# The first attention of a two-layer trunk: biased logits written to SBUF, a longer pipeline, and query tiles taken in turn from both ends of a head

## The chip, the cores and the metric
One core of a Trainium2 chip runs the whole program in one launch. The time is the device time of that core in microseconds (us). Three runs of the kernel before gave 2849.36 to 2856.4 us, median 2853.4 us.

## The reference
The trunk has two layers over 2048 tokens of width 1024, in float32. Only the first attention of layer 0 (A) is touched, with the two stages behind it:

```python
s = einsum('bhmqd,bhmkd->bhmqk', q, k) * ATTN_SCALE + bias          # 4 heads, 2 maps m each, 64 deep
p = softmax(where(kpos // 64 <= qpos // 64, s, -inf), axis=-1)
attn = p[:, :, 0] - lam * p[:, :, 1]
o = einsum('bhqk,bhkd->bhqd', attn, v)                              # v is 128 wide
o = rms_norm(o, subln_g) * (1.0 - lam_init)
mixed = concatenate([a_out * silu(ag), b_out * silu(bg)])
y = mixed @ w_out_even
```

The bias depends on the distance alone. Beyond the last 256 keys in front of the diagonal it is constant over a row, and the kernel keeps only what differs from that.

## The kernel before, in words
The program is a chain of stages, each a block of its own with a barrier behind it: `project` (layer 0), `diff_attn` (attention A, tiles named a_), `band_attn` (B, b_), `output` (o_), and the same for layer 1 with attention C (c_). Every engine's order inside a stage is written by hand, and semaphores join the engines.

`diff_attn` (L534) goes through 64 steps `(h, i)`, 4 heads by 16 query tiles of 128 rows. The mask is causal, so step i has n = i + 1 key tiles of 128. In a head there are 136 key tiles. `steps` is in rising order of i. For each step g and each of the two maps m:

- TensorE (`qk`, L645) writes the negated logits into `logits`, 5 PSUM banks of 512 columns used in a ring, in ceil(n / 4) parts, two matmuls a part (high and low halves).
- VectorE (`maxima`) takes the minimum of each part but the last by a reduction (L709), joins them (L716), and adds the bias to the last part and folds its minimum in with one custom instruction (L720), which writes the part back to PSUM in place.
- ScalarE (`exponentials`, L770) takes one exponential a part out of PSUM into `prob` in SBUF, with a partial row sum each.

For the step as a whole VectorE (`difference`) sums the partial sums (L728), forms a ratio (L729, L730) and computes `prob0 + ratio * prob1`, 512 columns at a time (L734). TensorE transposes the result tile by tile (L658) into two `turned` banks, ScalarE copies those to `prob_t` (L778), TensorE multiplies by v (L671), VectorE scales the result into `out` (L739) and ScalarE takes its squares (L784). The loops are shifted against each other: in iteration g TensorE does `qk(g, 0)`, `pv(g - 2)`, `qk(g, 1)`, `transposes(g - 1)`, and VectorE does `maxima(g, 0)`, `difference(g - 1)`, `maxima(g, 1)`, `output(g - 2)`.

After the 64 steps comes a tail: the RMS factors of all 64 tiles (L752 to L754 and L80 to L83), 64 scalings by them (L757), 64 transposes (L689), 16 copies (L803) and 4 stores of 1 MB on SyncE's queue (L621).

The keys, queries and values of a head are loaded by SyncE's queue (L598 to L616), 13 DMAs for each block of 512 tokens, into two sets of buffers. Heads 0 and 1 are loaded at the start, head h + 2 when the products of head h are done. TensorE waits for block b of a head where it first needs it, at step i = 4b.

`output` (L1137) multiplies the concatenated heads by the gates and projects. For B the division by the row sums is made here: GpSimd widens the inverse sums to 512 columns (L1175), TensorE transposes them (`spreads`, L1290, 4 transposes a token tile; 8 in layer 1, where all 16 heads are such), and VectorE multiplies the gates by them (L1252).

## Time and profile before

| | us |
|---|---|
| median of three runs | 2853.4 |
| the profiled execution | 2854.47 |
| its span | 2852.8 |
| granted TensorE clock, mean of the span | 0.969 |
| first matmul of attention A to the first DMA of attention B | 650.26 to 1076.19 |

All sums below are made against the profiled execution, whose time is 1.7 us above its span. Busy time counts the instructions themselves; an engine that waits for another is idle. Matmul durations in a timeline overlap: the cost of one in a row of many is the distance between starts.

### The profile page before, as it was taken

The numbers are of one execution on the slowest core, as the hardware profiler recorded it, in microseconds if no ns is written. First come the engines' busy times: TensorE is split into PE (matmuls) and PEld (weight loads), VectorE is DVE, ScalarE is ACT, GpSimd is POOL, SyncE is SP. The second block draws the span as 40 slices with busy tenths as digits, with TensorE's granted clock in tenths as the row PEclk, the third lists the DMA queues.
The fourth block names the chain that finished last, engine by engine and source line by source line (L and its number), as shares of the span: only waits on it lengthen the run. The fifth ranks groups of instructions, "written<-read, shape, count | busy, mean of one in ns | idle before, by whom it ended". The sixth has DMA issues, their size and how long they took to land. (4 is left out here: it accounts for less than half of the span.)

```text
span 2852.8 us, 44070 instructions
## 1 busy us (share of the span) xinstructions
PE 2617.7 (92%) x16264; PEld 2231.2 (78%) x16264; DVE 1244.4 (44%) x2881; ACT 914.0 (32%) x2357; POOL 310.1 (11%) x199
## 2 busy tenths in 40 slices
PE   5999999987888885979969999999996999999898
PEld 4788888986676664768858888888996888888687
DVE  6411111107889873745531111111111777777465
ACT  4211111006777763622121111111001555555121
POOL 1121212100000003100012122121110000100100
PEclk9999999998999997989989999999998999999899
DMA  5344522129315009765463343321225676774652
GB/s 170 120 137 134 164 72 85 50 62 195 82 24 103 1 31 235 183 212 212 171 214 116 117 128 111 103 78 63 61 61 118 156 182 160 177 173 95 196 210 78
DMA packets 237932, 359.53 MB, mean 126 GB/s; under 512 B 59604, under 2 KB 136832, under 8 KB 237232
## 3 DMA queue, kind: packets, MB, share of 16 engines
q1 hardware_dynamic: 222800, 309.33, 39.2%
q0 software_dynamic: 11104, 41.95, 5.1%
q10 hardware_dynamic: 3840, 5.77, 0.9%
q8 instruction: 115, 1.88, 0.3%
q14 instruction: 73, 0.60, 0.1%
HBM read 223.75 MB, written 138.70 MB: 127 GB/s over the span
## 5 line engine op out<-in xcount | busy, mean ns | idle before, releaser
L520 PE MATMUL p_acc<-p_h_hi,p_w_hi 128*128 128x512 f32 x1440 | 565.1, 392 | 11.2 <-DVE p_h_lo L464 11.2
L520 PE MATMUL p_acc<-p_h_hi,p_w_lo 128*128 128x512 f32 x1440 | 562.0, 390 | 0.0
L520 PE MATMUL p_acc<-p_h_lo,p_w_hi 128*128 128x512 f32 x1440 | 561.9, 390 | 0.0
L520 PEld LDWEIGHTS p_acc<-p_h_hi,p_w_hi 128*128 128x128 f32 x1440 | 271.4, 188 | 69.9 <-DVE p_h_lo L464 14.5
L520 PEld LDWEIGHTS p_acc<-p_h_hi,p_w_lo 128*128 128x128 f32 x1440 | 271.1, 188 | 57.0
L520 PEld LDWEIGHTS p_acc<-p_h_lo,p_w_hi 128*128 128x128 f32 x1440 | 271.4, 188 | 55.3
L235 DVE SCALAR_TENSOR_TENSOR p_lo_out<-p_acc,p_hi_out 128x512 fp32r<-128x512 f32 x116 | 80.0, 691 | 486.7 <-ACT p_hi_out L219 486.6
L1108 ACT ACTIVATE c_prob<-c_logits,c_neg_max 128x640 f32<-128x640 f32 (+4 forms) x256 | 185.1, 727 | 206.2 <-DVE c_neg_max L1089 206.1
L1089 DVE CUSTOM_DVE_ANT_0 c_logits<-c_logits,c_bias 128x640 f32<-128x640 f32 (+4 forms) x256 | 185.8, 761 | 122.2 <-PE c_logits L1020 111.2
L219 ACT ACTIVATE p_hi_out<-p_acc 128x512 fp32r<-128x512 f32 x116 | 69.4, 598 | 511.0 <-PE p_acc L520 493.5
L517 PE MATMUL p_acc<-p_w_hi,p_h_lo 128*128 128x256 f32 (+1 forms) x768 | 224.0, 292 | 0.0
L517 PE MATMUL p_acc<-p_w_lo,p_h_hi 128*128 128x256 f32 (+1 forms) x768 | 224.0, 292 | 0.0
L517 PE MATMUL p_acc<-p_w_hi,p_h_hi 128*128 128x256 f32 (+1 forms) x768 | 224.0, 292 | 0.0
L1305 PE MATMUL o_acc<-w_out_hi,o_m_hi 128*128 128x512 f32 x512 | 204.4, 399 | 7.5 <-DVE o_m_lo L1256 7.5
L645 PE MATMUL a_logits<-a_k,a_q 128*128 128x512 f32 (+3 forms) x640 | 175.9, 395 | 37.1 <-DMA a_v<-scr_v_a 18.8
L770 ACT ACTIVATE a_prob<-a_logits,a_neg_max 128x512 f32<-128x512 f32 (+3 forms) x320 | 195.8, 624 | 34.8 <-DVE a_neg_max L720 33.7
L1305 PE MATMUL o_acc<-w_out_lo,o_m_hi 128*128 128x512 f32 x512 | 201.6, 394 | 0.0
L1305 PE MATMUL o_acc<-w_out_hi,o_m_lo 128*128 128x512 f32 x512 | 201.6, 394 | 0.0
L1020 PE MATMUL c_logits<-c_k,c_q 128*128 128x384 f32 (+2 forms) x960 | 176.3, 324 | 25.7 <-DMA c_v<-scr_v 24.6
L1020 PEld LDWEIGHTS c_logits<-c_k,c_q 128*128 128x128 f32 x960 | 147.0, 192 | 51.1 <-DMA c_v<-scr_v 25.4
L238 DVE TENSOR_TENSOR p_f_out<-p_acc,p_sig 128x512 f32<-128x512 f32 x64 | 44.2, 691 | 303.9 <-ACT p_sig L221 303.9
L1053 PE MATMUL c_o<-c_prob_t,c_v 128*64 128x128 f32 x2240 | 154.3, 279 | 0.1
(152 smaller groups left out, 4019.5 us busy)
## 6 DMA issues: line engine op xcount, KB each, us to landing
scr_qh<-p_hi_out SPq DMA_DIRECT2D x116, 256.0 KB, 2.5
scr_ql<-p_lo_out SPq DMA_DIRECT2D x116, 256.0 KB, 2.9
scr_gt<-p_f_out SPq DMA_DIRECT2D x128, 128.0 KB, 1.9
p_w_raw<-in_w_in_odd POOLq DMA_DIRECT2D x16, 1024.0 KB, 6.8
c_k<-scr_qh SPq DMA_DIRECT2D x60, 256.0 KB, 8.3
c_k<-scr_ql SPq DMA_DIRECT2D x60, 256.0 KB, 10.0
o_o<-scr_ot SPq DMA_DIRECT2D x6, 2048.0 KB, 8.7
o_g<-scr_gt SPq DMA_DIRECT2D x6, 2048.0 KB, 13.7
```

The source lines that it names most:

```text
L219: nc.scalar.activation(hi_out[:, buf, :], ps[:, :], ACT.Copy, scale=kind[1]).then_inc(act_done, 1)
L235: nc.vector.scalar_tensor_tensor(out=lo_out[:, buf, :], in0=ps[:, :], scalar=kind[1], in1=hi_out[:, buf, :].bitcast(F32), op0=ALU.mult, op ...
L238: nc.vector.tensor_tensor(f_out[:, buf, :], ps[:, :], sig[:, buf, :], ALU.mult).then_inc(dve_done, 1)
L517: last = nc.tensor.matmul(acc[v % 4][:, 0:n], ht[:, c, k * P:(k + 1) * P], wt[:, half, c * n:(c + 1) * n], **flags)
L520: last = nc.tensor.matmul(acc[v % 4][:, :], wt[:, half, c * n + cc * P:c * n + (cc + 1) * P], ht[:, c, b * BLK:(b + 1) * BLK], **flags)
L645: last = nc.tensor.matmul(logits[n % RING][:, 0:tiles * P], q, k_sb[h % 2][m][:, at * P:(at + tiles) * P], start=s == 0, stop=s == 1)
L770: nc.scalar.activation(prob[g % 2][m][:, at * P:(at + tiles) * P], logits[n % RING][:, 0:tiles * P], ACT.Exp, bias=neg_max[:, j:j + 1], sc ...
L1020: last = nc.tensor.matmul(s_ps[:, lo:hi], q_sb[b][:, i * P:(i + 1) * P], k_sb[b][s][:, tile * P:tile * P + hi - lo], start=s == 0, stop=s ...
L1053: last = nc.tensor.matmul(o_ps[half * HD:(half + 1) * HD, at:at + P], v_sb[:, j // TILES % 2, tile_of(j + half) - w + 1 + t, :], prob_t[:, ...
L1089: nc.vector.tensor_tensor_reduce(out=to, in0=s, in1=bias[:, b, WIDE - w * P:WIDE + SPARE], scale=1.0, scalar=HIGHEST, op0=ALU.add, op1=ALU ...
L1108: nc.scalar.activation(prob[:, j, 0:n], source, ACT.Exp, bias=neg_max[:, j:j + 1], scale=-1.0, accum_out=sums[:, h, tile_of(k):tile_of(k) ...
L1305: last = nc.tensor.matmul(acc[u % 4][:, :], mt[:, t % 2, c, :], wt[:, c, half * BLK:(half + 1) * BLK], start=step == 0, stop=step == 3 * K ...
```

## The change
In `diff_attn`:

- `logits` is now a ring of 3 parts of 1024 columns (6 banks), and `turned` is one bank in place of two.
- A map has one part for up to 8 key tiles and two above that. The last part has 8 tiles. Every part goes through the custom instruction, which now writes to `prob` in SBUF: the first part is added to `zeros`, the last to the bias, padded with zeros to 1024 columns. TensorE waits for `moved`, that is for VectorE, where it waited for the exponentials before.
- ScalarE makes one exponential for the whole row of a map, in place in SBUF, and its sum is the row sum.
- `difference` works on pieces of 1024 columns. `prob` of map 0 has three buffers.
- The loops are shifted further: `transposes(g - 2)` and `pv(g - 3)` alternate, four tiles at a time, with `qk(g, 1)` in the middle.
- The steps of a head are ordered 15, 0, 14, 1, ..., 8, 7; in head 0 they are 0, 1, 2, 3, then 15, 4, 14, 5, ..., 10, 9. TensorE waits for the blocks of a head where a step first needs them.
- `out` has 8 slots. Every 4 steps its tiles are transposed, copied with the gain and stored by four DMAs of 64 KB. Loads of head h + 2 stand behind the stores of head h on SyncE's queue.
- The tail is gone. The RMS factors are computed at the start of `band_attn` and applied in the first `output`, by widening them along with B's inverse sums: two GpSimd copies and 8 transposes a token tile instead of one and 4, and a gate product of 1024 columns instead of 512.

```diff
-        bias = st.sb("bias", [P, A_HEADS, BLK])
-        prob = [[st.sb(f"prob{b}{m}", [P, SEQ]) for m in range(2)] for b in range(2)]
+        PART = 2 * BLK
+        bias = st.sb("bias", [P, A_HEADS, PART])
+        zeros = st.sb("zeros", [P, PART])
+        prob = [[st.sb(f"prob{m}{b}", [P, SEQ]) for b in range(3 - m)] for m in range(2)]
         prob_t = st.sb("prob_t", [P, 2, SEQ])
-        out = st.sb("out", [P, A_HEADS * TILES, P])
+        SLOTS = 2 * TPB
+        out = st.sb("out", [P, SLOTS, P])
+        out_t = st.sb("out_t", [P, 2, BLK])
...
-        RING = 5
-        logits = [st.ps(f"logits{i}", [P, BLK]) for i in range(RING)]
-        turned = [st.ps(f"turned{i}", [P, BLK]) for i in range(2)]
+        RING = 3
+        logits = [st.ps(f"logits{i}", [P, PART]) for i in range(RING)]
+        turned = st.ps("turned", [P, BLK])
...
+        def mixed(first, last):
+            tiles = range(first, last)
+            return [i for pair in zip(reversed(tiles), tiles) for i in pair][:len(tiles)]
+
+        steps = [(h, i) for h in range(A_HEADS) for i in (list(range(TPB)) + mixed(TPB, TILES) if h == 0 else mixed(0, TILES))]
...
+                last = min(n, PART // P)
+                parts[g, m] = []
+                for at, tiles in [(0, n - last)] * (n > last) + [(n - last, last)]:
...
+            load(0)
+            load(1)
+            for n in range(G // TPB):
+                h, r = divmod(n, NBLK)
+                sp.wait_ge(out_left, n + 1)
+                for t in range(TPB):
+                    i = steps[n * TPB + t][1]
+                    sp.dma_start(scr["ot"][h * P:(h + 1) * P, i * P:(i + 1) * P], out_t[:, n % 2, t * P:(t + 1) * P]).then_inc(stored[n % 2], 16)
+                if r == NBLK - 1 and h + 2 < A_HEADS:
+                    sp.wait_ge(pv_done, TILES * (h + 1))
+                    load(h + 2)
...
+                if m == 0:
+                    for n in needs[g]:
+                        pe.wait_ge(head_loaded[h % 2][n], 16 * LOADS * (h // 2 + 1))
+                for n, at, tiles in parts[g, m]:
+                    if n >= RING:
+                        pe.wait_ge(moved, n - RING + 1)
...
+                pe.wait_ge(diff_done, diffs[g][k // 2][0] + 1)
+                turned_free()
...
-            for g in range(G + 2):
-                for k in range(NBLK if g < G else 0):
-                    qk(g, 0, k)
-                for k in range(NBLK if g >= 2 else 0):
-                    pv(g - 2, k)
-                for k in range(NBLK if g < G else 0):
-                    qk(g, 1, k)
-                for k in range(NBLK if 1 <= g <= G else 0):
-                    transposes(g - 1, k)
...
+            for g in range(G + 5):
+                if g < G:
+                    qk(g, 0)
+                if g >= 4 and (g - 4) % TPB == TPB - 1:
+                    out_transposes((g - 4) // TPB)
+                for k in range(NBLK):
+                    if k == 2 and g < G:
+                        qk(g, 1)
+                    if 2 <= g < G + 2:
+                        transposes(g - 2, k)
+                    if 3 <= g < G + 3:
+                        pv(g - 3, k)
...
+                if m == 0 and g >= 3:
+                    dve.wait_ge(turned_done, turns[g - 3][-1][0] + 1)
+                to, start = prob[m][g % (3 - m)], HIGHEST
+                if len(parts[g, m]) > 1:
+                    n, at, tiles = parts[g, m][0]
                     dve.wait_ge(qk_done, n + 1)
-                    last = nc.vector.tensor_reduce(out=part_max[:, m, k:k + 1], in_=logits[n % RING][:, 0:tiles * P], axis=AX.X, op=ALU.min)
-                start = HIGHEST
...
-                    start = part_max[:, m, 3:4]
-                    link(nc.vector.tensor_reduce(out=start, in_=part_max[:, m, 0:len(earlier)], axis=AX.X, op=ALU.min))
+                    start = part_max[:, m:m + 1]
+                    nc.vector.tensor_tensor_reduce(out=to[:, at * P:(at + tiles) * P], in0=logits[n % RING][:, 0:tiles * P], in1=zeros[:, 0:tiles * P],
+                                                   scale=1.0, scalar=HIGHEST, op0=ALU.add, op1=ALU.min, accum_out=start).then_inc(moved, 1)
+                    dve.wait_ge(moved, n + 1)
                 n, at, tiles = parts[g, m][-1]
                 dve.wait_ge(qk_done, n + 1)
-                s = logits[n % RING][:, 0:tiles * P]
-                nc.vector.tensor_tensor_reduce(out=s, in0=s, in1=bias[:, h, BLK - tiles * P:BLK], scale=1.0, scalar=start,
-                                               op0=ALU.add, op1=ALU.min, accum_out=neg_max[:, j:j + 1]).then_inc(max_done, 1)
+                nc.vector.tensor_tensor_reduce(out=to[:, at * P:(at + tiles) * P], in0=logits[n % RING][:, 0:tiles * P], in1=bias[:, h, PART - tiles * P:PART],
+                                               scale=1.0, scalar=start, op0=ALU.add, op1=ALU.min, accum_out=neg_max[:, j:j + 1]).then_inc(moved, 1)
...
+                dve.wait_ge(exp_done, 2 * g + 2)
+                sums = row_sum[:, g % 2, :]
...
+                for n, at, tiles in diffs[g]:
...
+                    nc.vector.scalar_tensor_tensor(out=prob[0][g % 3][:, cols], in0=prob[1][g % 2][:, cols], scalar=ratio[:, 0:1],
+                                                   in1=prob[0][g % 3][:, cols], op0=ALU.mult, op1=ALU.add).then_inc(diff_done, 1)
...
-                for k, (n, at, tiles) in enumerate(parts[g, m]):
-                    nc.scalar.activation(prob[g % 2][m][:, at * P:(at + tiles) * P], logits[n % RING][:, 0:tiles * P], ACT.Exp,
-                                         bias=neg_max[:, j:j + 1], scale=-1.0, accum_out=part_sum[:, g % 2, m, k:k + 1]).then_inc(exp_done, 1)
...
+                act.wait_ge(moved, parts[g, m][-1][0] + 1)
+                p = prob[m][g % (3 - m)][:, 0:(i + 1) * P]
+                nc.scalar.activation(p, p, ACT.Exp, bias=neg_max[:, j:j + 1], scale=-1.0, accum_out=row_sum[:, g % 2, m:m + 1]).then_inc(exp_done, 1)
...
-            for g in range(G + 3):
+            for g in range(G + 5):
+                if g >= 4 and (g - 4) % TPB == TPB - 1:
+                    out_leaves((g - 4) // TPB)
+                for k in range(2 if 2 <= g < G + 2 else 0):
+                    leave(g - 2, k)
                 if g < G:
                     exponentials(g, 0)
-                if 1 <= g <= G:
-                    leave(g - 1)
+                for k in range(2, NBLK if 2 <= g < G + 2 else 2):
+                    leave(g - 2, k)
                 if g < G:
                     exponentials(g, 1)
...
+            if ssq is not None:
+                nc.vector.tensor_scalar(mean[:, :, :], ssq[:, :, :], 1.0 / P, EPS, ALU.mult, ALU.add).then_inc(mean_done, 1)
+                dve.wait_ge(root_done, 1)
+                link(nc.vector.reciprocal(rms[:, :, :], root[:, :, :]))
+                sharpen(nc, link, rms[:, :, :], mean[:, :, :], root[:, :, :])
...
+            if ssq is not None:
+                act.wait_ge(mean_done, 1)
+                nc.scalar.activation(root[:, :, :], mean[:, :, :], ACT.Sqrt).then_inc(root_done, 1)
...
+                if EARLIER:
+                    nc.gpsimd.tensor_copy(wide[:, t % 2, 0:EARLIER, :], rms[:, :, t:t + 1].to_broadcast([P, EARLIER, P])).then_inc(widened, 1)
+                nc.gpsimd.tensor_copy(wide[:, t % 2, EARLIER:KC, :].rearrange("p c (h d) -> p (c h) d", d=HD),
+                                      inv_sums[:, :, t:t + 1].to_broadcast([P, heads, HD])).then_inc(widened, 1)
...
+                pe.wait_ge(widened, (t + 1) * (2 if EARLIER else 1))
+                for c in range(KC):
+                    last = nc.tensor.transpose(spread[:, c, :], wide[:, t % 2, c, :], keep["ident"][:, :])
```

**TensorE, head 0, around the fifth step.** Before (a_logits are the two maps' logits, a_o the product with v); the fifth step is i = 4:
```order
L671 MATMUL a_o<-a_v,a_prob_t 128x128 [waits a_out_done,a_prob_t_done]
L671 MATMUL a_o<-a_v,a_prob_t 128x128
L645 MATMUL a_logits<-a_k,a_q 128x512 [waits a_exp_done]
L645 MATMUL a_logits<-a_k,a_q 128x512
L658 MATMUL a_turned<-keep_ident,a_prob 128x128 [waits a_prob_t_done,a_diff_done]
L658 MATMUL a_turned<-keep_ident,a_prob 128x128 x2
L645 MATMUL a_logits<-a_k,a_q 128x128 [waits a_exp_done,a_head_loaded0_1]
L645 MATMUL a_logits<-a_k,a_q 128x128
L645 MATMUL a_logits<-a_k,a_q 128x512 [waits a_exp_done]
```
Of the change, where the fifth step is i = 15:
```order
L669 MATMUL a_logits<-a_k,a_q 128x512
L690 MATMUL a_turned<-keep_ident,a_prob 128x128 [waits a_prob_t_done,a_diff_done]
L690 MATMUL a_turned<-keep_ident,a_prob 128x128
L712 MATMUL a_o<-a_v,a_prob_t 128x128 [waits a_prob_t_done]
L669 MATMUL a_logits<-a_k,a_q 128x512 [waits a_moved]
L669 MATMUL a_logits<-a_k,a_q 128x512
L669 MATMUL a_logits<-a_k,a_q 128x512 [waits a_head_loaded0_3,a_moved,a_head_loaded0_2,a_head_loaded0_1]
L669 MATMUL a_logits<-a_k,a_q 128x512 x3
```
The fifth step waited for block 1 alone, and now waits for blocks 1, 2 and 3; the transposes and products of the steps in front of it, which stand behind that wait, wait as well.

**VectorE, a step with 16 key tiles beside shorter ones.** Before (a_part_max holds the minima of parts, a_neg_max that of the row; the second row of each custom instruction reads its accumulator):
```order
L709 TENSOR_REDUCE a_part_max<-a_logits 128x1 x3
L716 TENSOR_REDUCE a_part_max<-a_part_max 128x1
L720 ISA a_logits,a_neg_max<-a_logits,a_bias,a_part_max 128x512
L720 ISA a_neg_max 128x1
L739 TENSOR_SCALAR a_out<-a_o,a_inv_sum 128x128
L720 ISA a_logits,a_neg_max<-a_logits,a_bias 128x128
L720 ISA a_neg_max 128x1
L728 TENSOR_REDUCE a_row_sum<-a_part_sum 128x2
L729 RECIPROCAL a_inv_sum<-a_row_sum 128x2
L730 SCALAR_TENSOR_TENSOR a_ratio<-a_row_sum,keep_nlam,a_inv_sum 128x1
L734 SCALAR_TENSOR_TENSOR a_prob<-a_prob,a_ratio 128x512 x4
```
Of the change:
```order
L749 ISA a_prob,a_part_max<-a_logits,a_zeros 128x1024
L749 ISA a_part_max 128x1
L754 ISA a_prob,a_neg_max<-a_logits,a_bias,a_part_max 128x1024
L754 ISA a_neg_max 128x1
L774 TENSOR_SCALAR a_out<-a_o,a_inv_sum 128x128
L754 ISA a_prob,a_neg_max<-a_logits,a_bias 128x640
L754 ISA a_neg_max 128x1
L761 RECIPROCAL a_inv_sum<-a_row_sum 128x2
L762 SCALAR_TENSOR_TENSOR a_ratio<-a_row_sum,keep_nlam,a_inv_sum 128x1
L766 SCALAR_TENSOR_TENSOR a_prob<-a_prob,a_ratio 128x1024 x2
L754 ISA a_prob,a_neg_max<-a_logits,a_bias 128x640
L754 ISA a_neg_max 128x1
```
Three reductions, a join and a 512-column instruction of a map became two instructions of 1024 columns, the sum of partial sums (L728) went, and four differences became two. The difference of the long step still comes after the first maxima of the next step, which is now a short one.

**TensorE, head 1, first step (i = 15), behind its `qk(g, 0)`.** Of the change:
```order
L690 MATMUL a_turned<-keep_ident,a_prob 128x128 [waits a_out_left,a_prob_t_done,a_diff_done]
L690 MATMUL a_turned<-keep_ident,a_prob 128x128 x3
L712 MATMUL a_o<-a_v,a_prob_t 128x128 [waits a_out_done,a_prob_t_done]
L712 MATMUL a_o<-a_v,a_prob_t 128x128 x3
L690 MATMUL a_turned<-keep_ident,a_prob 128x128 [waits a_out_left,a_prob_t_done,a_diff_done]
L690 MATMUL a_turned<-keep_ident,a_prob 128x128 x3
L712 MATMUL a_o<-a_v,a_prob_t 128x128 [waits a_prob_t_done]
L712 MATMUL a_o<-a_v,a_prob_t 128x128 x3
L669 MATMUL a_logits<-a_k,a_q 128x512 [waits a_moved]
L669 MATMUL a_logits<-a_k,a_q 128x512 x3
L669 MATMUL a_logits<-a_k,a_q 128x512 [waits a_moved]
L669 MATMUL a_logits<-a_k,a_q 128x512 x3
```
Each group of transposes now waits for the copy of the group in front of it (a_prob_t_done), since `turned` is one bank; before, it waited for the copy of the last but one.

## Rows read from the trace of the kernel before

**Rows 1.** Second head: stretch, us; busy PE, PEld, DVE, ACT, POOL; clock, DMA share, GB/s
```profile
757.00:857.00 100.00, 87.38 (x571) 70.31 (x572) 86.30 (x235) 74.85 (x232) 0.00 (x0) 1.00 0.33 75
```

**Rows 2.** Timeline of VectorE, longest step: start us, us, engine, line, operation, tiles
```profile
839.59 1.87 DVE L709 TENSOR_REDUCE a_part_max<-a_logits 128x1 f32<-128x512 f32 x3
...
841.68 0.76 DVE L720 CUSTOM_DVE_ANT_0 a_logits<-a_logits,a_bias,a_part_max 128x512 f32<-128x512 f32 x1
...
842.36 0.35 DVE L739 TENSOR_SCALAR a_out<-a_o,a_inv_sum 128x128 f32<-128x128 f32 x1
...
846.02 0.16 DVE L728 TENSOR_REDUCE a_row_sum<-a_part_sum 128x2 f32<-128x8 f32 x1 [2.77 <-ACT a_prob L770]
...
846.67 2.74 DVE L734 SCALAR_TENSOR_TENSOR a_prob<-a_prob,a_ratio 128x512 f32<-128x512 f32 x4
```

**Rows 3.** Groups of instructions by shape, 700 to 1160 us (busy us, mean ns)
```profile
L770 ACT ACTIVATE a_prob<-a_logits,a_neg_max 128x128 f32<-128x128 f32 x26 | 9.6, 368 | 6.8 <-DVE a_neg_max L720 6.4
...
L709 DVE TENSOR_REDUCE a_part_max<-a_logits 128x1 f32<-128x512 f32 x110 | 72.7, 684 | 15.4 <-PE a_logits L645 15.2
...
L720 DVE CUSTOM_DVE_ANT_0 a_logits<-a_logits,a_bias,a_part_max 128x512 f32<-128x512 f32 x82 | 62.2, 759 | 4.2 <-PE a_logits L645 1.0
...
L720 DVE CUSTOM_DVE_ANT_0 a_logits<-a_logits,a_bias 128x512 f32<-128x512 f32 x6 | 4.2, 696 | 0.8 <-PE a_logits L645 0.8
...
L720 DVE DVE_READ_ACCUMULATOR2_ANT a_neg_max<- 128x1 f32 x106 | 15.0, 141 | 0.0
...
L778 ACT ACTIVATE a_prob_t<-a_turned 128x512 f32<-128x512 f32 x102 | 58.1, 596 | 51.1 <-PE a_turned L658 51.0
...
L1108 ACT ACTIVATE b_prob<-b_shifted,b_neg_max 128x257 f32<-128x257 f32 x58 | 29.2, 504 | 28.2 <-DVE b_neg_max L1089 27.8
```

**Rows 4.** Timeline of ScalarE, two neighbouring exponentials
```profile
843.20 0.69 ACT L770 ACTIVATE a_prob<-a_logits,a_neg_max 128x512 f32<-128x512 f32 x1
...
843.86 0.70 ACT L770 ACTIVATE a_prob<-a_logits,a_neg_max 128x512 f32<-128x512 f32 x1
```

**Rows 5.** Timeline of TensorE beside them
```profile
838.33 2.07 PE L645 MATMUL a_logits<-a_k,a_q 128*128 128x512 f32 x8
840.24 1.03 PE L658 MATMUL a_turned<-keep_ident,a_prob 128*128 128x128 f32 x8
...
842.44 0.42 PE L645 MATMUL a_logits<-a_k,a_q 128*128 128x128 f32 x2
842.85 3.59 PE L671 MATMUL a_o<-a_v,a_prob_t 128*128 128x128 f32 x30
```

**Rows 6.** Start: timeline of TensorE; timeline of SyncE's queue
```profile
650.26 2.07 PE L645 MATMUL a_logits<-a_k,a_q 128*128 128x128 f32 x8 [18.84 <-DMA a_v<-scr_v_a]
...
666.29 0.59 SPq L616 DMA_DIRECT2D a_v<-scr_v_a  x1
```

**Rows 7.** Landing time of the value loads, 630 to 720 us (median us)
```profile
a_v<-scr_v_a SPq DMA_DIRECT2D x7, 256.0 KB, 9.2
```

**Rows 8.** Busy times just after the first matmuls; the column before DMA is the clock
```profile
655.00:660.00 5.00, 4.16 (x14) 2.59 (x13) 3.87 (x16) 2.39 (x7) 0.00 (x0) 0.50 1.10 210
```

**Rows 9.** End of A, start of B: timelines of TensorE, ScalarE, SyncE's queue and VectorE
```profile
1037.42 2.07 PE L645 MATMUL a_logits<-a_k,a_q 128*128 128x512 f32 x8
...
1071.21 0.69 ACT L803 ACTIVATE a_prob<-a_turned,keep_sub_g 128x512 f32<-128x512 f32 x1
...
1076.19 0.47 SPq L892 DMA_DIRECT2D b_q<-scr_qh  x1
...
1093.29 0.29 DVE L1089 CUSTOM_DVE_ANT_0 b_shifted<-b_logits,b_bias 128x129 f32<-128x129 f32 x1 [16.93 <-POOL b_bias L972]
```

**Rows 10.** Output stages: VectorE's timeline in the first, chain of waits in the second
```profile
1271.15 0.68 DVE L1252 TENSOR_TENSOR o_g<-o_g,o_spread 128x512 f32<-128x512 f32 x1
1271.86 1.23 DVE L1254 TENSOR_TENSOR o_o<-o_o,o_g 128x1024 f32<-128x1024 f32 x1
...
2740.00 0.87 PE o_spread L1290 x8
```

218 lines of the change are left out of this document (100 added, 118 removed).

## The prediction
> **What bounds the kernel now.** I read the busy times by stage first. While the second head of attention A runs [rows 1], TensorE is busy 87.4 us of 100, VectorE 86.3, ScalarE 74.9, with the clock at its full level (1.00, so 2.4 GHz). Three engines near their limit: the timelines say which wait ends last. In VectorE's [rows 2] the reader sees one instruction follow the other without a gap through the long step (839.59 to 842.36), and a wait of 2.77 us for ScalarE at 846.02, where a head ends: its 16-tile row is still in the exponentials while the next head's 1-tile steps offer nothing to do in between. TensorE and ScalarE wait for each other and for VectorE all along (ScalarE's copies stood idle 51.1 us for transposes between 700 and 1160 us, [rows 3]). So attention A is bound by VectorE, plus some 13 us at each change of head. Its two ends are bare: the first matmul waits 18.84 us for loads [rows 6], and from the last logits at 1037.42 to the first DMA of attention B at 1076.19 [rows 9] nothing of B runs.
>
> **VectorE, a head of 136 tiles.** A tile's width costs (1.23 - 0.68)/4 = 0.135 us in an operation that has nothing but width to add [rows 10]; I use 0.133, which makes 512 columns 0.53. What differs is the fixed part, taken as the distance between starts minus the width. The custom instruction of 512 columns with a start value in SBUF: 841.68 to 842.36, 0.68 - 0.53 = 0.15 us [rows 2]; without one it is 63 ns shorter (696 against 759 ns, [rows 3]), 0.08. Reductions: 1.87/3 = 0.62, fixed 0.09; the join behind them takes the rest to 841.68, 0.22. Differences: 2.74 for four, the last outlasting its slot by 0.08, so 0.665 each, fixed 0.13 [rows 2]. From 846.02 to 846.67 stand the three small ones, 0.65, of which L728 is 0.2. L739 is 0.3, its 0.35 less the overlap.
> Before: 136 x 3 tiles are 54.4 us; 48 reductions 4.3; 16 joins 3.5; 24 custom instructions with start value 3.6 and 8 without 0.6; 16 x 0.65 for ratios 10.4; 40 differences 5.2; outputs 4.8. Sum 86.8, against 86.3 in [rows 1]: the count holds.
> After: 54.4 again; 16 first parts, whose accumulator must be read before the next may start, 0.08 + 0.14 [rows 3] + 0.03 = 0.25 each, 4.0; 16 last parts with start value 2.4 and 16 single parts 1.3; ratios without L728 16 x 0.45 = 7.2; 24 differences 3.1; outputs 4.8. Sum 77. The write goes to SBUF instead of PSUM; the nearest row is B's, which does that, 257 columns, and its price I take as equal. The bounds are 0.06 us less or more an instruction, 2 to 3 us a head.
> Reductions become custom instructions here. By the rows that costs: 696 ns against 684 [rows 3], and the accumulator's 141 ns behind it, in all 16 x 0.17 = 2.7 us a head, which the count above holds. The other way round is among the rivals.
>
> **ScalarE.** Four times the columns make an exponential 0.69 us long in place of 0.37 [rows 3, 4], 0.107 us a tile. One of 512 columns repeats after 0.66 us [rows 4], 0.43 of it width, so 0.23 fixed; 80 of them become 32 of full rows, which takes 48 x 0.23 = 11 us off a head. Reading SBUF costs a little: 504 ns for 257 columns in B [rows 3] against 0.69 us less 255 columns' 0.21, that is 0.48, so 0.03 each and 1 us a head. Squares and copies stay; 4 copies with the gain, 0.7 each, come in from the tail. ScalarE has 74.9 - 11 + 1 + 2.8 = 68 us in a head.
>
> **TensorE** gets nothing off. Logits are 112 matmuls at (840.24 - 838.33)/8 = 0.24 and 48 narrower ones at 0.18 (0.2 for 128 columns), 35.5 us; 272 halves of products at 0.112 are 30.4; 136 transposes at 0.115, 15.6 [rows 5]. With 16 transposes from the tail 83 us. It becomes the longest.
>
> **How a head runs then.** I take two steps together, since the order makes every pair 17 tiles. The middle pair (9, 8): TensorE 10.4, VectorE 9.6, and ScalarE's row of 9 tiles (1.2 us) ends while VectorE does an output and the next maxima (1.7 us): TensorE's pace, say 10.6. The extreme pair (16, 1): the second exponential can start only when ScalarE has left the third and fourth copy, each waiting for TensorE in the single `turned` bank, some 0.5 us after the maxima; it takes 1.94 + 0.03; VectorE meanwhile has 0.5 us of work (an output and maxima of one tile). So it waits about 2 us on top of its 9.7: 11.7. In between 11.2, and a head 8 x 11.2 = **90 us**. The change of head costs nothing more, because each head now ends in middle steps.
>
> **The start.** The fifth step needs block 3 of head 0. Its last DMA is issued at 666.29 [rows 6] and lands 9.2 us later [rows 7], at 675.5; neither queue nor order of these loads changes. The first four steps, ten tiles, are long done. In the kernel before, steps of 5 to 8 tiles filled this time, so a wait of some 14 us is new. TensorE comes out of it cold: behind the first wait of the stage the clock was 0.50, 1.2 GHz, still at 655 to 660 [rows 8]. I charge 3 us, between nothing, were other engines the slower ones in this time, and 5, the 10 us from 650 to 660 at half pace.
> Loads of head 2 are now behind head 0's last stores, about three steps into head 1. An issue takes 0.59 us [rows 6], 52 of them with their gaps 33, and 9 to land: done some 63 us after head 1 starts, with 27 to spare. Hidden.
> The remaining 126 tiles of head 0 have fewer short steps and so less fixed cost: 78 us.
>
> **The end.** Behind the last logits (8 tiles): lag and maxima 2.3, exponential 1.2, ratio and difference 1.7, two rounds of four transposes and a copy 2.2, products 0.9, output, transposes and gain copy 1.5. From the last copy to B's first DMA it took 1076.19 - 1071.90 = 4.3 us with one 1 MB store behind it [rows 9]; four small stores add three issues of 0.6. Together 16 us. The RMS factors, with a square root and its table, lie in B's start, where VectorE waits 16.93 us for GpSimd's bias [rows 9] and ScalarE for VectorE: nothing, unless that bias came 5 us sooner.
>
> **The sum for A.** 675.5 + 3 + 78 + 3 x 90 + 16 = 1042.5, against 1076.2: -34.
> **First output stage.** TensorE bounds it, and gets 4 transposes a tile more. In layer 1, where there are eight, they take 0.87 us [rows 10], so 16 x 0.44 = 7. VectorE's gate product grows from 0.68 to 1.23 us [rows 10], which shows in the first tiles, +1. GpSimd's second copy is hidden except once. Together +8.
> The profiled execution took 2854.5: 2854.5 - 34 + 8 = 2828.5; the profiled execution lies 1.1 above the median, so **2827 us**.
>
> **The rivals.**
> *TensorE alone sets the pace* (20%). For it: after the change VectorE and ScalarE have 6 and 15 us a head in hand, and the ring holds 3 x 1024 columns. A head is then 83 us; heads and the rest of head 0 together count 3.87 heads, so 27 us less: 2800. Against it: the 2 us wait of VectorE at long rows has nothing ahead of it to fill.
> *No change* (13%). One `turned` bank makes copies and transposes take turns. If the products of a short neighbour, 0.23 us a tile, don't cover a 0.6 us copy, each of the 24 later copies of a head costs up to 0.3 us more than counted: 97 us a head, +27, and 2854.
> *Slower* (9%). The same place, worse: every later copy is a full round of transposes, copy and two signals, 1.15 us for 0.45, so 24 x 0.7 = 17 us on TensorE's 83, and in the 8 long steps the third copy stands behind a whole-row exponential of up to 2 us that cannot be split, half of it bare, 8 us less what overlaps: 104 a head, 2881. The point from which it decides is 97 us a head. For it: ScalarE already idles 51.1 us before those copies with two banks. Against it: `pv(g - 3)` now stands between them.
> *The exchange of reductions for the custom instruction gains* (3%). Then VectorE's 2.7 us a head turn from a cost into nothing or less; middle pairs keep TensorE's pace, so half counts: 3.87 x 1.4 = 5 us, 2822. Against it: 684 and 696 ns [rows 3]. The Trainium skill ("VectorE: DVE Perf Modes", Rules for kernel authors) calls `tensor_reduce` the slowest VectorE operation and advises to restructure where it is hot; by that rule this rival would be the case, and the rows speak against it.
> *The change doesn't do what it says*: the orders shown above have the wide instructions and both ends, so I give this nothing.
>
> **How the numbers follow.** The forecast has 55%, the exchange 3% inside it, with its own range 2812 to 2842 (a head 86 to 94). Whole range 2798 to 2856: from the TensorE case to just above no change; it leaves out the slow case and what lies below the TensorE case. Within 0.3%, about what a measurement can tell here, is 2845 to 2862. Faster: 0.55 + 0.03 + 0.20 = 0.78; same 0.13; slower 0.09.
>
> **What would show it.** Right: no matmul from about 661 to 675 and a clock of half behind it; a distance of 88 to 92 us between heads; VectorE's waits before L761 behind the longest rows, for the exponentials of L794; B's first DMA near 1042; first output tiles 11.8 us apart. Wrong: heads above 97 us with TensorE waiting on the copies of L803, a wait for head_loaded at heads 2 or 3, or a wide custom instruction above 1.3 us.

## The result, and the profile after

The changed kernel takes **2898.0 us** (median of 4 runs, 2892.8 to 2908.6) against 2852.4 for the one before (4 runs, 2849.4 to 2856.4): ratio 1.016, 95% interval 1.013 to 1.019. It is 46 us slower. The forecast was 2827, faster; the result lies outside its range. The profiled execution took 2892.8 us, 38 more than the profiled one of before.

| first instruction of, or event | before, us | after, us | later by |
|---|---|---|---|
| first logits of attention A | 650.3 | 650.6 | 0.3 |
| last logits of A (start of the last matmul) | 1039.1 | 1083.7 | 44.6 |
| first DMA of attention B | 1076.2 | 1100.6 | 24.4 |
| products of the first output stage | 1237.9 | 1264.0 | 26.1 |
| end of layer 1's projection with rows as tokens | 1990.6 | 2021.9 | 31.3 |
| first logits of attention C | 2186.5 | 2225.2 | 38.7 |
| end | 2852.8 | 2891.1 | 38.3 |

So attention A, which was to give 34 us, lost 24; attention B lost 2, the output stage 5 and the second projection 7. First the second head, as in [rows 1]; a head (last output to last output) now takes 107 us, before 99.5:

```profile
786.00:893.00 107.00, 89.32 (x587) 78.48 (x585) 76.60 (x169) 66.30 (x140) 0.00 (x0) 0.95 0.40 80
```

VectorE was counted at 77 us a head and has 76.6; ScalarE at 68 and has 66.3. The work came out as counted, and none of the three engines is full. The clock is 0.95, where it was 1.00. Waits between 650 and 1110 us (us in total, times, longest):

```profile
ACT a_prob_t L803 <- PE a_turned L690: 108.4, 114, 20.6
...
DVE a_prob L754 <- PE a_logits L669: 81.0, 70, 18.6
...
PE a_logits L669 <- DMA a_v<-scr_v_a: 36.7, 2, 18.5
...
PE a_turned L690 <- ACT a_out_t L809: 26.9, 15, 2.2
...
DVE a_inv_sum L761 <- ACT a_prob L794: 23.0, 27, 1.7
```

VectorE now waits for logits: 81.0 us at L754 and 30.8 at L749, where L720 and L709 of before had 31.6 and 15.8 (18.6 and 19.0 of these are the first wait of the stage, and 18.9 at L749 is the wait for block 3). TensorE waits 15 times for L809, the copy with the gain that stands behind each group of output transposes (the 16 groups of `out_transposes` and `out_leaves`). The outputs show its rhythm: in a mixed head they come mostly 5.3 to 6.4 us apart, but each fourth interval is 6.9 to 10.7 (around the change of head the others reach 8.0). One such place, in the timeline of all engines (start us, us):

```profile
863.75 0.34 DVE L774 TENSOR_SCALAR a_out<-a_o,a_inv_sum 128x128 f32<-128x128 f32 x1
863.87 1.26 ACT L794 ACTIVATE a_prob<-a_prob,a_neg_max 128x1152 f32<-128x1152 f32 x1 [1.19 <-DVE a_neg_max L754]
...
864.15 0.66 PE L698 MATMUL a_turned<-keep_ident,a_out 128*128 128x128 f32 x4 [0.97 <-DVE a_out L774]
...
865.12 0.29 ACT L816 ACTIVATE a_square<-a_out 128x128 f32<-128x128 f32 x1
...
865.41 0.67 ACT L809 ACTIVATE a_out_t<-a_turned,keep_sub_g 128x512 f32<-128x512 f32 x1
...
866.23 0.63 PE L690 MATMUL a_turned<-keep_ident,a_prob 128*128 128x128 f32 x4 [1.42 <-ACT a_out_t L809]
...
870.03 1.22 DVE L754 CUSTOM_DVE_ANT_0 a_prob<-a_logits,a_bias 128x1024 f32<-128x1024 f32 x1 [2.78 <-PE a_logits L669]
```

Read it as a chain. TensorE waits 0.97 us for the newest output; its four transposes fill the only `turned` bank; the copy stands behind a whole-row exponential of 1152 columns and a square; only then may TensorE turn the next probabilities, 1.42 us later, and VectorE stands idle 2.78 us before the next logits reach it. This is the mildest kind of place: the exponential in front of the copy is one of 9 tiles; in the same head others have 15, 13 and 11.

The start, answering to [rows 6, 8]: TensorE's timeline, then busy times by stretch (the column before DMA is the clock):

```profile
650.56 2.71 PE L669 MATMUL a_logits<-a_k,a_q 128*128 128x128 f32 x10 [18.46 <-DMA a_v<-scr_v_a]
...
675.28 3.75 PE L669 MATMUL a_logits<-a_k,a_q 128*128 128x512 f32 x8 [18.22 <-DMA a_v<-scr_v_a]
```
```profile
660.00:675.00 15.00, 0.00 (x0) 0.00 (x0) 0.00 (x0) 0.00 (x0) 0.00 (x0) 0.50 1.10 231
675.00:680.00 5.00, 4.72 (x14) 3.87 (x15) 2.05 (x3) 0.23 (x1) 0.00 (x0) 0.50 1.08 239
```

The block came at 675.3 (forecast 675.5), with the clock at half, 1.2 GHz, behind it. The shapes, answering to [rows 3] (700 to 1160 us; busy us, mean ns):

```profile
L754 DVE CUSTOM_DVE_ANT_0 a_prob<-a_logits,a_bias,a_part_max 128x1024 f32<-128x1024 f32 x60 | 77.0, 1284 | 13.2 <-PE a_logits L669 11.9
...
L803 ACT ACTIVATE a_prob_t<-a_turned 128x512 f32<-128x512 f32 x107 | 63.4, 593 | 64.7 <-PE a_turned L690 64.7
...
L794 ACT ACTIVATE a_prob<-a_prob,a_neg_max 128x2048 f32<-128x2048 f32 x6 | 12.0, 2002 | 3.5 <-DVE a_neg_max L754 3.5
...
L809 ACT ACTIVATE a_out_t<-a_turned,keep_sub_g 128x512 f32<-128x512 f32 x16 | 10.7, 671 | 2.9 <-PE a_turned L698 2.9
...
L754 DVE DVE_READ_ACCUMULATOR2_ANT a_neg_max<- 128x1 f32 x113 | 9.3, 83 | 0.0
```

Twice the columns cost 1284 ns, under the 1.3 named as a sign of error. The end, answering to [rows 9]: the last logits (timeline of TensorE), B's first DMA (SyncE's queue), and B's start (VectorE, TensorE, VectorE):

```profile
1082.88 1.17 PE L669 MATMUL a_logits<-a_k,a_q 128*128 128x512 f32 x4
```
```profile
1100.65 0.48 SPq L924 DMA_DIRECT2D b_q<-scr_qh  x1
```
```profile
1111.20 0.55 DVE L1114 RECIPROCAL rms_a<-b_root 128x64 f32<-128x64 f32 x1 [10.32 <-ACT b_root L1173]
...
1112.97 1.22 PE L1052 MATMUL b_logits<-b_k,b_q 128*128 128x128 f32 x4 [16.60 <-DVE b_logits L1119]
...
1115.63 0.29 DVE L1134 CUSTOM_DVE_ANT_0 b_shifted<-b_logits,b_bias 128x129 f32<-128x129 f32 x1 [2.73 <-POOL b_bias L1004]
```

L1119 writes the spare logits column of B; it stands behind the RMS factors on VectorE.

### The profile page after: what moved, and what is told of

Its sections match the earlier page's. It is cut to its first block and busy times, and to the rows that moved or that the text cites. A ratio compares the mean times of both kernels' runs of the same rounds, so it can differ in the third digit from the quotient of the medians.

```text
span 2891.1 us, 43546 instructions
## 1 busy us (share of the span) xinstructions
PE 2625.7 (91%) x16328; PEld 2267.2 (78%) x16328; DVE 1199.3 (41%) x2561; ACT 868.8 (30%) x1973; POOL 323.1 (11%) x216
## 5 line engine op out<-in xcount | busy, mean ns | idle before, releaser
L520 PE MATMUL p_acc<-p_h_hi,p_w_hi 128*128 128x512 f32 x1440 | 565.5, 393 | 16.6 <-DVE p_h_lo L464 16.6
L517 PE MATMUL p_acc<-p_w_lo,p_h_hi 128*128 128x256 f32 (+1 forms) x768 | 224.7, 293 | 2.6 <-issue 2.6
L517 PE MATMUL p_acc<-p_w_hi,p_h_hi 128*128 128x256 f32 (+1 forms) x768 | 225.0, 293 | 2.2 <-issue 2.2
L517 PE MATMUL p_acc<-p_w_hi,p_h_lo 128*128 128x256 f32 (+1 forms) x768 | 224.8, 293 | 0.0
L669 PE MATMUL a_logits<-a_k,a_q 128*128 128x512 f32 (+3 forms) x640 | 164.9, 391 | 36.7 <-DMA a_v<-scr_v_a 36.7
L794 ACT ACTIVATE a_prob<-a_prob,a_neg_max 128x128 f32<-128x128 f32 (+15 forms) x128 | 153.4, 1199 | 76.8 <-DVE a_neg_max L754 76.8
L712 PE MATMUL a_o<-a_v,a_prob_t 128*128 128x128 f32 x1088 | 158.2, 294 | 6.8 <-DVE a_out L774 6.5
```

The lines of the kernel that those rows point to most:

```text
L517: last = nc.tensor.matmul(acc[v % 4][:, 0:n], ht[:, c, k * P:(k + 1) * P], wt[:, half, c * n:(c + 1) * n], **flags)
L520: last = nc.tensor.matmul(acc[v % 4][:, :], wt[:, half, c * n + cc * P:c * n + (cc + 1) * P], ht[:, c, b * BLK:(b + 1) * BLK], **flags)
L669: last = nc.tensor.matmul(logits[n % RING][:, first * P:(first + some) * P], q, k_sb[h % 2][m][:, (at + first) * P:(at + first + some) * P ...
L712: last = nc.tensor.matmul(o_ps[:, :], prob_t[:, g % 2, t * P:(t + 1) * P], v_sb[:, h % 2, t, :], start=t == 0, stop=t == i)
L794: nc.scalar.activation(p, p, ACT.Exp, bias=neg_max[:, j:j + 1], scale=-1.0, accum_out=row_sum[:, g % 2, m:m + 1]).then_inc(exp_done, 1)
```

## The experiments

Times are medians; each ratio is to the kernel before, with its 95% interval. "Heads" are the distances from the last output of one head to that of the next, for heads 1, 2 and 3 (head 3 has no head behind it, which makes it shorter where it ends on short or middle rows), and the end of head 0 is its last output, at L774 or its like. "A" is the time from the first logits of attention A to the first DMA of attention B. Heads and A come from the one profiled execution of each kernel; what lies outside A varies too, so a difference of two times and that of two A's need not agree.

| kernel | us | ratio | head 0 ends | heads | A |
|---|---|---|---|---|---|
| before | 2852.4 | 1 | 755.1 | 99.6, 99.5, 98.7 | 425.9 |
| changed | 2898.0 | 1.016 (1.013 to 1.019) | 785.7 | 106.9, 107.5, 95.2 | 450.1 |
| e1 no groups | 2845.0 | 0.997 (0.996 to 0.998) | 783.5 | 96.1, 95.7, 84.4 | 412.6 |
| e2 groups late | 2873.8 | 1.006 (1.004 to 1.008) | 786.4 | 101.2, 99.2, 90.9 | 433.1 |
| e3 own bank | 2854.3 | 1.000 (0.999 to 1.001) | 780.2 | 96.1, 94.6, 85.1 | 410.3 |
| e4 rising | 2833.9 | 0.994 (0.992 to 0.996) | 752.8 | 96.8, 98.4, 96.1 | 398.4 |
| e5 own bank, rising | 2827.0 | 0.991 (0.990 to 0.993) | 752.4 | 93.1, 93.1, 92.5 | 386.2 |
| e6 head 0 rising | 2869.9 | 1.006 (1.005 to 1.008) | 760.2 | 104.0, 108.0, 97.7 | 426.7 |
| e7 own bank, head 0 rising | 2829.6 | 0.993 (0.991 to 0.995) | 758.8 | 93.9, 94.5, 85.1 | 388.5 |
| e8 before, mixed | 2890.6 | 1.013 (1.011 to 1.015) | 757.1 | 112.5, 114.4, 105.0 | 465.8 |
| e9 = e6, short rows first | 2852.5 | 1.000 (0.999 to 1.001) | 756.9 | 101.2, 100.6, 94.2 | 410.2 |
| e10 = e9, groups late | 2875.9 | 1.009 (1.007 to 1.010) | 758.6 | 110.0, 109.2, 99.7 | 432.0 |
| e11 = e5, spare column first | 2828.1 | 0.992 (0.990 to 0.993) | 751.9 | 93.1, 93.1, 92.4 | 386.1 |
| e12 own bank, zigzag | 2813.1 | 0.986 (0.984 to 0.988) | 759.0 | 78.0, 101.3, 76.0 | 369.8 |
| e13 = e7, two banks | 2813.8 | 0.987 (0.985 to 0.989) | 753.7 | 90.1, 90.2, 79.7 | 369.1 |
| e14 = e7, narrow copies | 2816.5 | 0.987 (0.985 to 0.989) | 759.0 | 89.8, 89.9, 80.2 | 373.5 |
| e15 changed, zigzag | 2828.6 | 0.992 (0.990 to 0.994) | 762.7 | 82.3, 105.8, 80.2 | 384.4 |
| e16 two banks, zigzag | 2802.6 | 0.984 (0.982 to 0.985) | 755.4 | 75.6, 99.9, 73.5 | 361.1 |
| e17 two banks, rising | 2820.2 | 0.990 (0.988 to 0.991) | 750.4 | 90.8, 90.8, 90.1 | 372.4 |

**The groups of output turning: e1, e2, e3.** e1 removes both calls in the loops and stores the tiles unturned, so its result is not the reference's and only its time counts (`...` marks lines left out; two waits change along with the calls):

```diff
-                if g >= 4 and (g - 4) % TPB == TPB - 1:
-                    out_transposes((g - 4) // TPB)
...
-                if g >= 4 and (g - 4) % TPB == TPB - 1:
-                    out_leaves((g - 4) // TPB)
...
-                    sp.dma_start(scr["ot"][h * P:(h + 1) * P, i * P:(i + 1) * P], out_t[:, n % 2, t * P:(t + 1) * P]).then_inc(stored[n % 2], 16)
+                    sp.dma_start(scr["ot"][h * P:(h + 1) * P, i * P:(i + 1) * P], out[:, (n * TPB + t) % SLOTS, :]).then_inc(stored[n % 2], 16)
```


> The turning of the output tiles inside the loop is left out (16 groups of four transposes and 16 copies with the gain); the stores take the tiles as they are, so the result is not the reference's. Theory 1 (each group breaks the pipeline: TensorE waits for the newest output, loses its lead, then its copy stands behind a whole-row exponential; about 3.5 us each): the long interval in every four steps (7 to 10.7 us) falls to about 6, a head takes about 93 us instead of 107, first attention ends about 50 us sooner, the kernel takes about 2845 us. Theory 2 (the order, a long row beside a short one, sets the pace with the whole-row exponential): only the 1.3 us of work per group goes, a head takes at least 102 us, the kernel at least 2880 us.

The groups cost 53 us by the times and 37.5 by A, so 2.3 to 3.3 us each for 1.3 us of work. A head is 11 us shorter, as the first theory said. The intervals between outputs show where. In the second head the four groups cost 3.7, 3.6, 1.5 and 1.5 us against the same intervals of e1 (6.0, 5.6, 5.4, 5.9), and they stand behind exponentials of 15, 13, 11 and 9 tiles. In the third head the group behind 11 tiles costs 3.0 instead of 1.5. The two places have the same instructions and the same waits of TensorE (0.63 and 1.63 us); only the clock differs. The interval of the second head, then that of the third (PE alone; the next number is the clock):

```profile
839.41:846.34 6.93, 4.90 (x39) 1.00 0.15 40
947.40:955.83 8.43, 6.39 (x39) 0.80 0.11 31
```

So one fall of the granted clock costs 1.5 us here. In the mixed heads of the changed kernel it falls at seven of the twelve groups (0.80 to 0.82 over the interval, once 0.68), at both groups behind 15 and 13 tiles in each head. At 1.5 us each, that is an estimate of some 10 of the 33 us by which these three heads are longer than e1's; the rest is the waits themselves.

e2 has `g - 5` in the place of `g - 4` in both conditions.

> The same groups of four transposes and their copies, one step of the loop later on TensorE and ScalarE, so that TensorE no longer waits for an output that VectorE has just made. Theory 1a (the wait for the newest output is what costs): most of the loss comes back, a head about 97 us, the kernel about 2858 us. Theory 1b (the shared transpose bank costs: the copy still stands behind the second exponential of the step before, and everything after it on TensorE waits): a head stays at 104 to 107 us, the kernel at 2885 us or more. Theory 2 (the order): no change, 2898 us.

24 us of it come back, 17 by A: between the theories. The step of one changes two things at once, as e9 shows.

e3 turns each tile alone, ahead of the next row's products, into columns 128 to 255 of the bank that holds the products, and VectorE copies it out:

```diff
                 if k == 0 and g >= 1:
-                    pe.wait_ge(out_done, g)
+                    out_transpose(g - 1)
...
+                if g >= 4:
+                    dve.wait_ge(pv_done, g - 2)
+                    out_leave(g - 4)
                 if g >= 3:
                     output(g - 3)
+            out_leave(G - 1)
```


> Each output tile is turned by itself into spare columns of the bank of the products, just before the next row's products, and copied out by VectorE (64 copies of 128 columns, about 0.2 us each, 13 us of VectorE in all) instead of 16 copies of 512 by ScalarE from the shared transpose bank. Theory 1: the groups' stalls go and VectorE's 13 us come: a head 96 to 98 us, the kernel about 2860 us. Theory 2 (the order sets the pace): VectorE's added work is on the path, a head 110 us, the kernel about 2910 us.

44 us gone (40 by A), the outputs complete, although VectorE has 3.3 us a head more to do (79.8 us of 96): its work is not on the path of a mixed head.

**The order and the start: e4, e5, e6, e7.** One line is changed: `for i in range(TILES)` for all heads (e4, e5), or for head 0 alone (e6, e7).

> The changed kernel with every head's rows in rising order again; all else as changed. Theory 1: a head still takes 100 us or more, since the groups of output transposes stay; only the wait for block 3 of head 0 goes (about 20 us with the cold clock and the late outputs), the kernel about 2875 us. Theory 2 (the order): heads fall to 92 us or less, the first wait goes too, the kernel about 2830 us. Theory 3 (the mixed order helps as forecast, by about 6 us a head): heads 112 us, the kernel about 2900 us.

e4 came near the 2830 us of its second theory, but its heads take 96 to 98 us and not the 92 that went with it.

> The changed kernel with only head 0 in rising order, heads 1 to 3 mixed as in the change. Head 0's last output came at 785.7 us with the mixed order and at 752.8 with the rising one. If all of that is the wait for block 3 and what follows from it: about 30 us sooner, the kernel about 2868 us, heads 1 to 3 as changed (107, 107, 95 us). If the loss of the start is made good in the next head (its loads set the pace): less than 10 us, 2890 us.

e6 prices the start: 28 us between 2898.0 and 2869.9, 25 between e3 and e7, and 23 and 22 by A. Against e4 the mixed heads 1 to 3 then cost 36 us, 28 of them in A, although nothing but their order differs.

> Output tiles turned in the bank of the products and copied by VectorE, and every head's rows in rising order. If what the groups of output turning cost (about 11 us a head in the mixed order) and what the mixed order costs are separate: rising order and shared bank give 2834, so this gives 2834 - 40 = about 2795 us, a head 86 to 88 us. If the two are one cost (in the mixed order the group falls on tight steps, in the rising order it is mostly hidden): a head 92 to 95 us, the kernel 2820 to 2834 us.

> Output tiles turned in the bank of the products, head 0 rising, heads 1 to 3 mixed. Sum of the two costs found (44 us for the groups, 28 to 30 us for the start): about 2825 us, with heads of 95, 95 and 85 us. Against the same kernel with all heads rising it tells what the mixed order is worth by itself: the forecast's theory was some 3 us a head in favour of the mixed order.

The sums of e5's first case failed: with rising rows the groups cost 7 us (e4 against e5), with mixed rows 40 (e6 against e7). The 7 are too few for A: there it is 12 us, and 38 with mixed rows. Heads 1 to 3 alone, with twelve groups, give 12.6 us (291.3 against 278.7) and 36.2 (309.7 against 273.5), so 1.0 and 3.0 us a group. The difference lies mostly behind A, where the second projection of e4 took 4 us less (last section). Without the shared bank the two orders are equal, 2827.0 and 2829.6. So in this pipeline there is not one cost of the order and another of the groups, but one of both together.

**Which row the copy stands behind: e9, e10.** In the change's order the groups fall on odd steps, so that L809 is always behind the second exponential of a *long* row. e9 exchanges the two rows of each pair; e10 moves its groups one step later.

```diff
-            return [i for pair in zip(reversed(tiles), tiles) for i in pair][:len(tiles)]
+            return [i for pair in zip(tiles, reversed(tiles)) for i in pair][:len(tiles)]
```


> Head 0 rising, in heads 1 to 3 each pair of rows begins with the short one (1, 16, 2, 15, ...) in place of the long one; the groups of output turning stay where the change has them, so that their copy now stands behind the exponential of a short row, and the next step after it is a short one. Compared with head 0 rising and long rows first (2869.9 us). Theory A (what the copy stands behind decides, 1 to 2 us of it at each group): heads of 98 to 101 us, the kernel about 2848 us. Theory B (TensorE's wait for an output just made, whatever the row): heads stay at 104 to 108 us, the kernel within 6 us of 2870.

> As the run with short rows first, and the groups one step later on TensorE and ScalarE, so that the copy stands behind a long row's exponential again, but no output has just been made. Theory A: the gain of short rows first is lost again: heads 104 us or more, the kernel about 2870 us. Theory B: heads 98 us, the kernel about 2846 us or less, as one step later gave 24 us with long rows first.

This closes a square. With the copy behind a long row: 2869.9 (e6) and 2875.9 (e10). Behind a short one: 2852.5 (e9) and 2846 (an estimate: e2's 2873.8 less the 28 of the start). By A it is 426.7 and 432.0 against 410.2 and 409.7 (433.1 less 23.4). One step later helps by 24 us in one order and hurts by 23 in the other, so the wait for the newest output is a small part. TensorE's waits in 770 to 1050 us, e9 first and then e10:

```profile
PE a_turned L690 <- ACT a_out_t L809: 10.8, 11, 1.3
```
```profile
PE a_turned L690 <- ACT a_out_t L809: 21.8, 10, 2.5
```

1.0 against 2.2 us each (e2 has 0.9, e6 1.8). Times the 12 groups of the mixed heads that is 14 of the 23 us. The rest goes with the clock: between 880 and 980 us its mean is 0.98 in e9, 0.94 in e10, 0.92 in e6 and 1.00 in e2. In the changed kernel TensorE was busy 0.33 us of the 2 from 894 to 896, and from 896 to 902 the clock was 0.50, 1.2 GHz. That such a fall costs time of its own is what the pair of intervals under e1 shows; no run varied the clock alone.

**The mixed order in the old pipeline: e8.** The kernel before, with the step list of e6, waits for blocks as in the change, and outputs kept by row number.

> The kernel before with heads 1 to 3 in the mixed order and nothing else changed (head 0 rising, so no wait at the start). If the mixed order levels the work as the change means it to: the 13 us at each head's end shrink, a head 95 us or less, the kernel about 2840 us. If the mixed order costs in itself (a short row's round trip beside a long row's work): a head 100 us or more, the kernel 2855 us or more.

38 us slower (40 by A). My reading is that with a pipeline of two steps each short row leaves the long one's round trip bare; no run varies the depth alone. From 870 to 985 us TensorE waits for the differences of VectorE 13.1 us, against 3.9 in a head of before:

```profile
PE a_turned L668 <- DVE a_prob L744: 13.1, 8, 2.9
```

**The single transpose bank: e13, e14, e17.** Without groups a mixed head still took 94 to 96 us, not 90. e13 takes `RING = 2` for the logits and two `turned` banks used in turn; e14 cuts each copy of L803 to its first 128 columns, so its result is not the reference's.

> Output tiles in the bank of the products, head 0 rising, heads 1 to 3 mixed (2829.6 us, heads of 94 us), with two transpose banks, paid for with one of the three logits buffers. If the single transpose bank is what holds a mixed head at 94: heads of 90 us or less, the kernel about 2817 us. If the logits buffers are needed more: heads of 100 us or more, the kernel at 2845 us or more, and the bank stays open.

> The same kernel (2829.6 us) with each copy out of the transpose bank cut to its first 128 columns (the rest of the turned probabilities stays zero, so the result is not the reference's): about 0.3 us off each of some 40 copies a head, on ScalarE and in the round trip. If the round trip over the single bank holds the head: 40 x 0.3 = up to 12 us a head less, at least down to VectorE's 84 to 86 us, the kernel about 2808 us. If it does not: 2 us a head or less, the kernel at 2824 us or more.

Both give a head of 90 us. The second head of e7, then of e13 (columns as in [rows 1]):

```profile
853.00:947.00 94.00, 83.08 (x582) 73.25 (x582) 79.24 (x184) 63.42 (x136) 0.00 (x0) 1.00 0.44 90
```
```profile
844.00:934.00 90.00, 83.59 (x584) 73.43 (x584) 78.79 (x184) 63.17 (x137) 0.00 (x0) 1.00 0.43 94
```

The same work in 4 us less. e14 gave 13 of the 21 us that were expected of it. In such a head TensorE's waits for the copy fell from 8.8 us in 14 waits to 0.7 in 3, and three logits buffers were more than needed.

> The same with all heads rising. With one bank rising rows stood at 2827.0, mixed ones at 2829.6 us. If the single bank held the mixed order back more than the rising one: 2820 to 2827 us, so that the mixed order is worth 6 to 13 us as the change means it. If it held both alike: about 2811 us.

With two banks the mixed order stands at 2813.8 us against 2820.2, but the intervals of the two ratios overlap (0.985 to 0.989, 0.988 to 0.991), and by A it is 3 us (369.1 against 372.4). What there is lies at the end of the stage: a head inside the loop takes 90.1 us mixed and 90.8 rising; from the first logits of A to the last ones the mixed order took 353.2 us and the rising one 349.1, and from there to B's first DMA 15.9 against 23.4.

**B's start: e11.** The block with the RMS factors is put behind the memsets of the spare column.

> The version of output tiles in the bank of the products and rising rows (2827.0 us), with the spare logits column of the second attention set before the RMS factors instead of behind them. Prediction's term (the RMS factors at this start cost nothing, bias and loads hide them): TensorE's first product comes some 4 us sooner, its second still waits for the block that lands at the same time, the kernel at 2827 us, within 1 us. Rival (TensorE's wait of 16.4 us for that column is on the path): 4 to 5 us sooner, 2822.5 us.

TensorE's first product comes 2.5 us sooner (37.2 to 34.7 us after the last logits of A), and the last logits of B start at 1181.3 against 1181.7. The 16.6 us wait that looks so large in the profile cost nothing in the end, as the expectation's first case said: the bias and the second load end as late.

**The best version: e12, e15, e16.** `range(TILES) if h % 2 == 0 else reversed(range(TILES))`: equal rows meet at each change of head, and the stage drains on short rows.

> Output tiles in the bank of the products; heads 0 and 2 rising, heads 1 and 3 falling (long rows meet at one head change, short ones at the next, and the stage ends with short rows). If a change between long and short rows costs the pipeline time (6 us at the change from rising to mixed, as seen) : the two changes long to short go, the end drains on short rows, 8 to 12 us gained on 2827: about 2817 us. If short rows meeting each other only lengthen the stretch that is bound by round trips: the same, 2827 us.

> The changed kernel with nothing but the order changed: heads 0 and 2 rising, heads 1 and 3 falling. With rising rows the groups of output turning cost 7 us in all, with mixed rows 40. If that holds here: 2813 + 7 = about 2820 us. If falling heads bear them badly: 2835 us or more.

> Output tiles in the bank of the products, two transpose banks and two logits buffers, heads 0 and 2 rising, 1 and 3 falling. With one transpose bank the zigzag order gave 2813.1 us, with two banks the mixed order went from 2829.6 to 2813.8. If the two gains add: about 2800 us. If both recover the same waits: 2810 to 2813 us.

e12 gains 14 us on e5, 16.4 by A. Of these 14.9 are behind the last logits of A (24.9 us to B's first DMA in e5, 10.0 in e12) and 1.4 before them; e16 against e17 shows the same (23.4, then 10.1). So the end on short rows carries it, and no run shows a gain of the equal rows at the changes of head. Changing only the order in the changed kernel (e15) turns +46 into -24 us; the groups cost 15 us there (against e12), more than the 7 that its expectation took. e16 is the fastest: 2802.6 us, by the ratio 1.65% below the kernel before, with the last output at 1004.4 us against 1052.9.

## Why the prediction was wrong, point by point

- **"How a head runs then: 90 us."** This step failed: 107. It counted the output turning as 16 transposes on TensorE and 4 copies on ScalarE a head, 1.9 and 2.8 us of *work*, and gave it no place. Its place decides: in the shared bank, on an odd step, behind a long row's exponential. e1 gives 11 us a head for it. A further 4 to 6 us a head are the single bank (e7 against e13). With both gone a mixed head takes 90.1 us (e13), and its pairs 10.7 to 12.6 us, where 10.6 to 11.7 were forecast. So the count of engines and pairs held; a synchronisation of three engines was left out of it, and with it the falls of the clock behind its waits, for which the forecast had a term at the start only.
- **Size of the miss in A.** B's first DMA came at 1100.6 instead of 1042.5, 58 us. The three mixed heads took 309.6 us, against 260.0 in e13, which runs as forecast: 50. The end took 17.0 us behind the last logits' start at 1083.7, forecast 16: 1. Some 7 lie in head 0.
- **"The start."** Block 3 at 675.3 and the half clock: right. Against a rising head 0 the whole costs 25 to 28 us by the times and 22 to 23 by A, not the 17 named (14 of wait and 3 of clock): the outputs of steps 1 to 3 also stood behind TensorE's wait (658.3, then 684.0 us), so the pipeline had to fill again behind it.
- **"The change of head costs nothing more."** Right for mixed heads among themselves (94.5 and 90.2 us in e7 and e13 include it). Between rising and mixed it costs 6 us (head 0 ends at 758.8 in e7, 752.4 in e5).
- **VectorE, ScalarE, TensorE.** 76.6, 66.3 and, without the groups' disturbance, 83.6 us (e13, output transposes included), against 77, 68 and 83: right.
- **Loads of head 2, RMS factors.** Hidden, as forecast: only two waits for A's loads, both in head 0; e11 for the factors.
- **"First output stage, +8."** From its first product to the end of the token projection 5.2 us more. Its price was too high by 3; another 7.4 us came where nothing was forecast (below).
- **The rival "slower" (2881).** Right in direction and in its place, the single bank and the whole-row exponential, wrong in what stands there: it charged every later copy of probabilities 0.7 us (17 us a head) and the third copy's place behind the exponential, 21 us a head over TensorE's 83. Those copies cost 4 to 6; with them and the start, but without the output copies, the kernel is at no change (e3, 2854.3 us, heads of 85 to 96 us, under its point of 97). It was the output copies, which no rival named. I gave it 9%; the two waits it spoke of were in the rows, a third user of the bank was in the diff.
- **The exchange of reductions for custom instructions.** 1284 ns for 1024 columns with a start value and 83 for the accumulator behind it, 1367 in all, against 2 x 684 = 1368 for two reductions: the same. VectorE was not the bound either, so no run shows a gain from the exchange. The page of the Trainium skill that was weighed ("VectorE: DVE Perf Modes", Rules for kernel authors) is therefore not tested here.

## What to carry to other kernels

Work that moves from a tail into a pipelined loop must be given a place, not only a sum: ask which bank it takes, which engine must come by before the bank is free, and behind which instruction of that engine the release stands. A long instruction that cannot be split (here a whole-row exponential) makes that place a matter of which step it falls on, so the same four transposes and one copy cost 1.0 us with rising rows and 3.0 with mixed ones (heads 1 to 3). And levelling the work by the order gave nothing inside the loop here: in the old pipeline it lost 38 us (e8), with one bank it made no difference, with two a head was 0.7 us shorter. What paid was to end the stage on short rows, some 15 us. Last, price a recurring wait of TensorE above its own length: one fall of the clock behind it cost 1.5 us.

## What the runs showed of the hardware that was not expected

Reading VectorE's accumulator took 141 ns behind a custom instruction that writes to PSUM [rows 3], and 83 ns where it writes to SBUF. The granted clock fell inside attention A in the kernels with long idle stretches of TensorE (0.90 to 0.97 over a mixed head: changed, e6, e8, e10) and stayed at 0.98 to 1.00 in the others. A mean of 0.80 instead of 1.00 made the same interval 8.43 us long instead of 6.93 (under e1).

In the second projection the changed kernel shows a stall that the one before does not, though its code is the same: TensorE's waits, and the busy times of the stretch (PE alone; the next number is the clock):

```profile
PE p_acc L517 <- issue: 4.8, 2, 2.6
```
```profile
2112.00:2116.00 4.00, 3.08 (x26) 1.00 0.19 38
2116.00:2120.00 4.00, 0.70 (x2) 0.67 0.18 38
2120.00:2124.00 4.00, 3.41 (x17) 0.50 0.02 4
```

Two holes in which the profile names no wait, then half the clock: 7.4 us in all. From the first product of the output stage to the first logits of C it took 948.6 us before, 951.8 to 961.2 in the kernels with the change's output stage, and 948.3 in e8, which has the old one. 5 of it are the output stage. Most of the rest is the second projection (L517): 184.4 to 184.5 us before and in e1, e4 and e8, 188 to 192 in the others. Why its holes come in some kernels and not in others stays open.
